# Latent x tiles loaded transposed and scaled by columns, in the token phase of a diffusion-transformer layer

## What is computed

```python
def rmsnorm(x, g):
    y = xf * lax.rsqrt(jnp.mean(xf * xf, axis=-1, keepdims=True) + EPS)
    return (y * g.astype(jnp.float32)).astype(x.dtype)

def modulate(x, g, shift, scale):
    return rmsnorm(x, g) * (1.0 + scale) + shift

h_lat = modulate(x, g_attn[i], sh1, sc1)
h_ctx = modulate(ctx, g_attn[i], csh1, csc1)
# project(): z = h @ w_in (1024 x 1184), split into cq, ckv, kr, qs, ks, vs;
# q_m = rmsnorm(cq) @ w_uq, kv = rmsnorm(ckv) @ w_ukv, RMS norms and rotary on q and k
```

## Time and profile before

| what | us |
|---|---|
| median of 3 timed runs | 1397.72 (1397.13 to 1399.58) |
| profiled execution | 1399.78 |
| its span (first to last instruction) | 1398.0 |
| TensorE busy | 1357.5 |
| VectorE busy | 914.6 |
| ScalarE busy | 692.6 |
| GpSimd busy | 487.1 |

### The profile page before, as it was taken

The page is one execution under the profiler, slowest core; times in us unless marked ns, Lnnn a source line. Parts: engine busy times, 40 slices in busy tenths (PEclk is TensorE's granted clock), DMA queues, the critical chain, the costliest instruction groups (busy, mean ns, idle before and its releaser), DMA issues.

```text
span 1398.0 us, 18825 instructions
## 1 busy us (share of the span) xinstructions
PE 1357.5 (97%) x7262; PEld 1149.4 (82%) x7262; DVE 914.6 (65%) x1284; ACT 692.6 (50%) x1343; POOL 487.1 (35%) x321
## 2 busy tenths in 40 slices
PE   5899997999999999999999999999999999999999
PEld 1688987999899988988887888888888888888887
DVE  1878776777777877875774646547564654746463
ACT  2755655788778777972223424333332433333240
POOL 2766553121299992501102303132050323205010
PEclk8999998999999999999999999999999999999999
DMA  9555658433365646301123112121211212121013
GB/s 377 192 162 160 177 159 286 129 89 86 115 199 144 190 131 191 71 1 61 31 76 121 31 31 90 31 75 31 62 44 30 91 31 75 30 62 44 15 61 121
DMA packets 121576, 143.42 MB, mean 103 GB/s; under 512 B 8184, under 2 KB 103288, under 8 KB 118672
## 3 DMA queue, kind: packets, MB, share of 16 engines
q1 hardware_dynamic: 121232, 142.18, 32.6%
q0 software_dynamic: 256, 0.05, 0.0%
HBM read 108.38 MB, written 31.74 MB: 100 GB/s over the span
## 4 chain that ended last, share of the span: by engine, by line
PE 70%; DVE 11%; POOL 7%; ACT 6%; DMA 4%; issue 1%; SPq 1%; DVEq 0%; ACTq 0%; POOLq 0%
PE f_ps L2062 24%; PE f_ps L2331 19%; PE o_ps L1770 6%; PE a_ps L1422 4%; PE a_ps L1438 3%; PE f_ps L2347 3%; POOL l_wg L1349 3%; ACT s_pr L1519 3%; POOL l_gate L1351 3%; PE t_ps L956 2%; PE a_ps L1468 2%; DVE s_nmx L1604 2%; PE t_ps L945 1%; DMA t_wm<-in_w_mod 1%; DMA l_v<-scratch_v 1%
## 5 line engine op out<-in xcount | busy, mean ns | idle before, releaser
L2062 PE MATMUL f_ps<-h,f_w 128*128 128x512 f32 x1536 | 358.0, 389 | 0.4 <-DVE h L1836 0.2
L2062 PEld LDWEIGHTS f_ps<-h,f_w 128*128 128x128 f32 x1536 | 288.1, 188 | 60.7 <-DVE h L1836 0.7
L2261 DVE TENSOR_TENSOR mix<-mix,f_ps 128x512 f32<-128x512 f32 x196 | 128.7, 683 | 152.9 <-PE f_ps L2331 152.9
L2102 POOL TENSOR_TENSOR f_w<-f_w,f_g 128x1024 f32<-128x1024 f32 x30 | 77.0, 2590 | 390.2 <-DMA f_w<-in_w_mlp 342.7
L2139 ACT ACTIVATE f_a<-f_ps 128x512 f32<-128x512 f32 x64 | 38.2, 597 | 254.7 <-PE f_ps L2062 254.7
L2331 PE MATMUL f_ps<-f_bh,f_al 128*128 128x512 f32 x392 | 152.5, 389 | 0.0
L2331 PE MATMUL f_ps<-f_bh,f_ah 128*128 128x512 f32 x392 | 152.5, 389 | 0.0
L2331 PE MATMUL f_ps<-f_bl,f_ah 128*128 128x512 f32 x392 | 152.5, 389 | 0.0
L1618 DVE TENSOR_TENSOR l_pT<-a_ps,l_pT 128x512 fp32r<-128x512 f32 (+1 forms) x192 | 108.9, 594 | 54.0 <-ACT l_pT L1529 53.9
L1422 PE MATMUL a_ps<-l_k,l_q 96*128 96x512 f32 (+1 forms) x576 | 136.5, 366 | 1.6 <-DMA l_v<-scratch_v 1.1
L956 PE MATMUL t_ps<-w_in,t_h 128*128 128x416 f32 (+2 forms) x600 | 125.7, 355 | 0.3 <-DVE w_in L719 0.3
(11 more groups left out here) (223 smaller groups left out, 2425.1 us busy)
## 6 DMA issues: line engine op xcount, KB each, us to landing
l_wg<-in_w_mod SPq DMA_DIRECT2D x8, 2048.0 KB, 8.0
f_w1r<-in_w_mlp SPq DMA_DIRECT2D x32, 512.0 KB, 4.0
f_w<-in_w_mlp SPq DMA_DIRECT2D x16, 1024.0 KB, 5.0
t_wm<-in_w_mod SPq DMA_DIRECT2D x8, 1024.0 KB, 12.5
scratch_k<-t_kT SPq DMA_DIRECT2D x20, 384.0 KB, 3.7
l_k<-scratch_k SPq DMA_DIRECT2D x8, 960.0 KB, 10.6
scratch_q<-t_qT SPq DMA_DIRECT2D x16, 384.0 KB, 3.9
l_q<-scratch_q SPq DMA_DIRECT2D x8, 768.0 KB, 6.3
```

The lines of the kernel that those rows point to most:

```text
L2062: last = nc.tensor.matmul(ps[:, b, :], w1[:, g % 2, w, k, :], h2[x][:, k, half * HB:(half + 1) * HB], start=(k == 0 and i == 0), stop=(k = ...
L2261: V.tensor_tensor(x, x, ps[:, bank_of(i, t), :].rearrange("p (k c) -> p k c", c=P), ALU.add).then_inc(added, 1)
```

## The change

Context tiles keep their way. Latent tiles (t >= 2) change:

- The host adds an input `x_cols`, x per tile with the model dimension on partitions (8 blocks of 128x128). SP loads it into `xT[t % 2]` (`load_xT`, `next_xT`); the plain x is still loaded for its squares.
- TensorE doesn't turn x. Its fill "x" is one 128x128 matmul that turns a broadcast of the inverse-RMS column, so that the inverse stands along columns in every partition. It stands behind the first k of chunk 1, before "s"; before, "x0" and "x1" stood behind chunk 2.
- VectorE scales `xT` in eight instructions of 128 columns, one for each block, by a per-partition scale from `mods` and the inverse row in PSUM; the last one counts `emptied`. It later makes the low part from SBUF in one instruction of 1024 (`low_x`), into `lT[t % 2]`.
- GpSimd adds the shift from `mods`, broadcast along columns. ScalarE makes the high part from SBUF in one instruction of 1024 (`high_x`), in `hT[t % 2]`; `project` waits for `h_lo`.
- The latent scale and shift rows are not spread; four transposes of `mo` and one copy make `mods` (128x16).
- In turn 1, `scale_x(2)` moves from behind `inverses(0)` to behind `c_variances(1)`.
- The stores at the program's end count one semaphore, not four.

```diff
@@ -253,16 +258,19 @@
     slot = {}
     for i in range(-1, NT + 1):
         order = [("sk", 0), ("k0", 0), ("k1", 0)] if i == NCT else []
-        order += ([("s", i - 1)] if lat(i - 1) else []) + [("sk", i - 1)] if i > 1 else []
-        turned = [(k, i - 1) for k in (("k0", "k1", "q0", "q1") if lat(i - 1) else ("k0", "k1"))] if i > 1 else []
         here = [("c", i)] if 0 <= i < NT else []
-        order += here + turned if lat(i) else turned + here
-        order += [("x0", i + 1), ("x1", i + 1)] if i + 1 < NT else []
+        ahead = [("x", i + 1)] if 0 < i < NT - 1 else []
+        if i < 2:
+            order += here + ahead + ([("x0", i + 1), ("x1", i + 1)] if i < 1 else [])
+        else:
+            order += ahead + ([("s", i - 1)] if lat(i - 1) else []) + [("sk", i - 1)] + here
+            order += [(k, i - 1) for k in (("k0", "k1", "q0", "q1") if lat(i - 1) else ("k0", "k1"))]
         for f in order:
             slot[f] = len(slot)
 
-
-    spread_bank = (5, 6, 7, 3, 4, 5, 6, 7)
+    read_at = {f: n for n, f in enumerate(f for f in slot if f[0] != "x")}
+    spread_bank = (5, 6, 7, 3)
+    MB = 4
     JOBS = ["a0", "a1", "kv", "r0", "r1", "r2", "r3", "uq"]
     kv_bank = lambda t: UB if t == 1 else UB + 2
 
...
@@ -342,8 +353,16 @@
             sp.dma_start(wm[k], A["w_mod"][0, k * P:(k + 1) * P, 0:2 * D]).then_inc(wm_loaded[k], 16)
 
         def next_x(i):
-            sp.wait_ge(emptied, slot["x1", i] + 1)
+            sp.wait_ge(x_squared, i + 1)
+            if i < NCT:
+                sp.wait_ge(emptied, slot["x1", i] + 1)
             load_x(i + 2)
+
+        def next_xT(i):
+            sp.wait_ge(z_ready, z_at(i) + (3 if lat(i) else 1))
+            if i:
+                sp.wait_ge(xT_loaded, 16 * i)
+            load_xT(i + 2)
 
         sp.dma_start(cc[:, :, :], A["c_cols"]).then_inc(c_loaded, 16)
         sp.dma_start(ident[:, :], A["ident"]).then_inc(ident_loaded, 16)
...
@@ -403,13 +427,15 @@
             return tmp
 
         def add_shift(t):
-            pool.wait_ge(h_scaled, t)
-            if t == 1:
-                pool.wait_ge(spread_copied, 4)
-            if t == NCT:
-                pool.wait_ge(spread_copied, 8)
-            shift = shift_l if lat(t) else shift_c
-            G.tensor_tensor(xr[:, t % 2, :], xr[:, t % 2, :], shift[:, :], ALU.add).then_inc(h_ready, 1)
+            if lat(t):
+                pool.wait_ge(emptied, slot["x", t] + 1)
+            else:
+                pool.wait_ge(h_scaled, t)
+            if lat(t):
+                G.tensor_tensor(xT[t % 2][:, :, :], xT[t % 2][:, :, :], bc(mods[:, 0:8], P), ALU.add).then_inc(h_ready, 1)
+                return
+            pool.wait_ge(spread_copied, 4)
+            G.tensor_tensor(xr[:, t % 2, :], xr[:, t % 2, :], shift_c[:, :], ALU.add).then_inc(h_ready, 1)
 
         def rotate_keys(t):
 
...
@@ -505,12 +531,15 @@
 
         def copy_spread(n):
 
-            dst = (scale_l, shift_l)[n % 2] if n >= 4 else (scale_c, shift_c)[n % 2]
+            dst = (scale_c, shift_c)[n % 2]
             f = n // 2 % 2
             act.wait_ge(spread, n + 1)
-            if n < 4:
-                act.wait_ge(h0_ready, n // 2 + 1)
+            act.wait_ge(h0_ready, n // 2 + 1)
             nc.scalar.activation(dst[:, f * BANK:f * BANK + BANK], ps[:, spread_bank[n], :], ACT.Copy).then_inc(spread_copied, 1)
+
+        def high_x(t):
+            act.wait_ge(h_ready, t)
+            nc.scalar.activation(hT[t % 2][:, :, :], xT[t % 2][:, :, :], ACT.Copy).then_inc(h_hi, 1)
 
         def hi_fill(kind, t):
             n = slot[kind, t]
...
@@ -663,14 +689,19 @@
                     att.first_exp()
                 if lat(i - 1):
                     hi_fill("q0", i - 1)
-                    hi_fill("q1", i - 1)
+            if 1 < i < NT - 1:
+                high_x(i + 1)
+            if i > 1 and lat(i - 1):
+                hi_fill("q1", i - 1)
             if i < NT and not lat(i):
                 hi_fill("c", i)
             if lat(i) and i < NT:
                 copy_z(i, 2)
-            if i + 1 < NT:
-                hi_fill("x0", i + 1)
-                hi_fill("x1", i + 1)
+            if i == 0:
+                hi_fill("x0", 1)
+                hi_fill("x1", 1)
+            if i == 1:
+                high_x(2)
             if i == 0:
                 square_x(2, stn[:, 0, 26:27])
             if i == 1:
...
@@ -687,14 +718,22 @@
         link = Chain(dve, v_chain)
 
         def scale_x(t):
-            r = stx[:, t:t + 1] if t < 2 else inv[:, (t - 2) % 2, 26:27]
-            scale = scale_l if lat(t) else scale_c
-            if t == 1:
-                dve.wait_ge(spread_copied, 4)
-            if t == NCT:
-                dve.wait_ge(spread_copied, 8)
-            V.scalar_tensor_tensor(out=xr[:, t % 2, :], in0=xr[:, t % 2, :], scalar=r, in1=scale[:, :],
+            if lat(t):
+                dve.wait_ge(filled, slot["x", t] + 1)
+                dve.wait_ge(xT_loaded, 16 * (LATS(t) + 1))
+                for k in range(KC):
+                    x = xT[t % 2][:, k, :]
+                    ins = V.scalar_tensor_tensor(out=x, in0=x, scalar=mods[:, 8 + k:9 + k], in1=ps[:, slot["x", t] % 2, 0:P],
+                                                 op0=ALU.mult, op1=ALU.mult)
+                ins.then_inc(emptied, 1)
+                return
+            dve.wait_ge(spread_copied, 4)
+            V.scalar_tensor_tensor(out=xr[:, t % 2, :], in0=xr[:, t % 2, :], scalar=stx[:, t:t + 1], in1=scale_c[:, :],
                                    op0=ALU.mult, op1=ALU.mult).then_inc(h_scaled, 1)
+
+        def low_x(t):
+            dve.wait_ge(h_hi, t - 1)
+            V.tensor_tensor(lT[t % 2][:, :, :], xT[t % 2][:, :, :], hT[t % 2][:, :, :].bitcast(F32), ALU.subtract).then_inc(h_lo, 1)
 
         def modulate_first():
 
...
@@ -863,8 +905,6 @@
                 link.reach()
                 variances(i - 1)
                 inverses(i - 1)
-                if i == 1:
-                    scale_x(2)
                 scale_s(i - 1)
                 if lat(i - 1):
                     scale_q(i - 1)
...
@@ -900,9 +940,13 @@
             if i < NT and not lat(i):
                 lo_fill("c", i)
                 c_variances(i)
-            if i + 1 < NT:
-                lo_fill("x0", i + 1)
-                lo_fill("x1", i + 1)
+            if i == 0:
+                lo_fill("x0", 1)
+                lo_fill("x1", 1)
+            if i == 1:
+                scale_x(2)
+            if 0 < i < NT - 1:
+                low_x(i + 1)
             if i == 0:
                 low_weights("r0")
             if i == 1:
...
@@ -919,7 +963,10 @@
             n = slot[kind, t]
             if n >= 2:
                 pe.wait_ge(emptied, n - 1)
-            if kind[0] == "x":
+            if kind == "x":
+                pe.wait_ge(inv_ready, t - 1)
+                parts = [inv[:, (t - 2) % 2, 26:27].to_broadcast([P, P])]
+            elif kind[0] == "x":
                 f = int(kind[1])
                 if t:
                     pe.wait_ge(h_ready, t)
...
@@ -1025,32 +1074,31 @@
         project_first()
         for i in range(NT + 1):
             if 0 < i < NT:
-                pe.wait_ge(emptied, slot["x1", i] + 1)
+                if lat(i):
+                    pe.wait_ge(h_lo, i - 1)
+                else:
+                    pe.wait_ge(emptied, slot["x1", i] + 1)
                 project(i, 0, {1: ("sk", 0), 3: ("k0", 0), 5: ("k1", 0)} if i == NCT else {})
-            if i == 0:
-                for n in range(4, 8):
-                    spread_row(n)
             if i < NT and not lat(i):
                 fill("c", i)
-                fill("x0", i + 1)
-                fill("x1", i + 1)
                 if i == 0:
+                    fill("x0", 1)
+                    fill("x1", 1)
                     pe.wait_ge(w_lo, JOBS.index("kv"))
-                    pe.wait_ge(spread_copied, 8)
+                else:
+                    fill("x", 2)
                 pe.wait_ge(emptied, slot["c", i] + 1)
                 up_kv(i)
             elif i < NT:
                 if i == NCT:
                     pe.wait_ge(w_lo, JOBS.index("r3"))
+                ahead = {0: ("x", i + 1)} if i + 1 < NT else {}
                 if lat(i - 1):
-                    project(i, 1, {2: ("s", i - 1), 5: ("sk", i - 1)})
+                    project(i, 1, ahead | {2: ("s", i - 1), 5: ("sk", i - 1)})
                     project(i, 2, {1: ("c", i), 2: ("k0", i - 1), 3: ("k1", i - 1), 4: ("q0", i - 1), 6: ("q1", i - 1)})
                 else:
-                    project(i, 1, {4: ("sk", i - 1)})
+                    project(i, 1, ahead | {4: ("sk", i - 1)})
                     project(i, 2, {1: ("c", i), 3: ("k0", i - 1), 5: ("k1", i - 1)})
-                if i + 1 < NT:
-                    fill("x0", i + 1)
-                    fill("x1", i + 1)
                 pe.wait_ge(emptied, slot["c", i] + 1)
                 if i == NCT:
```

53 lines of the change are left out of this document (33 added, 20 removed).

## The result

The changed kernel takes 1407.73 us (median of 4 runs, 1406.67 to 1409.96), the kernel before 1398.65 us beside it (1397.13 to 1399.74). The ratio is 1.0068, with a 95% interval of 1.0053 to 1.0083: slower by 9.1 us, where 5.6 were forecast, inside the range. The span of the profiled run is 1408.0 us (before 1398.0), its mean granted clock 0.987 (0.988).

The account below looks back on a forecast made before the run. TensorE, busy for 97% of the span, was taken as the bound, with VectorE's queue on the path at the start. Start +3.5 and six tiles +2.1 gave +5.6 us on the median of 1397.72: 1403.3 us, range 1396.5 to 1410.

Parts of the forecast that it names:

- Sign and order of the causes: Token phase: slower by 5.6 us, +3.5 from the start and +2.1 from six tiles; chance of slower 0.69.
- The tile: Regular latent tiles: 1.15 us later for the sk wait, 0.81 earlier without transposes; +0.35 a tile, +2.1 for six.
- TensorE's q at 14.25 us in: Latent tile: TensorE's transposes of q come 14.25 us into the tile, which was 13.1.
- takes the same 2.38 us: Latent tile: GpSimd's shift of x was to keep its 2.38 us and start no later.
- Rival (a): Latent tiles: x emptied so early that sk never waits; tiles give 4.3 us, ending at 1394.9; chance 0.13.
- The start: Ahead of the regular tiles: the chain of scalings, shift, copy and subtraction delays `project(2, 0)`; +3.5 us (+1.5 to +5.5).
- I add 0.4 for the slow clock there and at 40 to 47 us: Start: TensorE's lower clock after idle ahead of `project(2, 0)` and at 40 to 47 us costs 0.4 us.
- SP is held no longer than before: nothing: SP's load queue: the added 512 KB `x_cols` load per tile, behind the spill of q, costs nothing.
- Less 0.8 for the transposes: Start, ahead of `project(3, 0)`: the removed transposes save 0.8 us, bringing the delay from +3.9 to +3.1.
- Rival (d): Latent tiles: the 1.3 us wait lowers TensorE's clock, 2 us more a tile, total 1415; chance 0.07.
- the nearer row: Earlier trace: an idle of 1.15 us left the clock at 1.00; nearer to the tile's 1.3 than the 2.00 us idle.
- Rival (c): Tile's end: VectorE's subtraction of 1024 meets GpSimd's rotation of q, say 0.8 us a tile, total 1408; chance 0.11.

Follow-up runs that it names:

- e5_warm: Changed kernel plus eight 128x512 matmuls that nobody reads in TensorE's idle ahead of `project(2, 0)`; ratio 1.0048 to the kernel before.
- c0_again: The changed kernel run once more, unchanged; ratio 1.0060 to the kernel before.
- e2_x2_early: Changed kernel with x(2)'s inverse filled inside `project(1, 0)` and x(2) scaled before the low half of v(0); ratio 1.0035 to the kernel before.
- e10_hold: e9_tail plus twelve matmuls that nobody reads in the first stage; ratio 1.0014 to the kernel before.
- e9_tail: Changed kernel with x(2)'s scaling, x(3)'s load and c(1) earlier, unread spreads restored, other moves, tile scalings ahead of k's scaling; ratio 0.9997 to the kernel before.

## Why the forecast was right, and where it was short

**Sign and order of the causes: right.** Both places were named, and both mechanisms are in the trace as written: the two-bank wait of sk in six tiles, and the chain of scalings, shift, copy and subtraction ahead of `project(2, 0)`.

**The tile: +0.35 forecast, +0.46 found.** The scalings span 2.15 us (2.2 forecast), sk stands 8.54 us into the tile (8.5), and the wait is 1.15 us (1.3), since the spread inverse and the rest put TensorE there at 7.4 and not at 7.2. The step that was short is "TensorE's q at 14.25 us in": it stands at 14.45 and waits 0.29 us for k's low parts. ScalarE begins k0 at 12.58 (12.5 forecast), copies for 0.84 us to 166.86; VectorE begins at 166.96 and has two parts done at 167.82, TensorE begins at 167.89. The hand-overs between engines, about 0.1 us each, were left out of the sum. Over the six tiles it is +2.5 us where +2.1 was forecast, since one tile of before took 20.55.

**GpSimd's shift "takes the same 2.38 us": wrong, by luck harmless.** It took 1.90 us with the shift read as eight broadcast columns instead of a full second tensor. VectorE's work beside it isn't the reason: next to the same low part of w_uq it took 2.37 us before (at 71.78) and 1.90 after (at 81.65). At the start this is 0.5 us less on the chain; in the tile nobody waits for it.

**The low part of vs.** Rival (a) rested on VectorE and GpSimd holding each other up less. They do (0.33 us instead of 1.86), but the time comes free behind the scalings, where VectorE then waits for ScalarE's c: it could not help sk.

**The start: +3.5 forecast, about +6.2 found.** From `project_first` to `project(2, 0)` the sum was nearly right: 27.64 us in both traces of the changed kernel, 23.46 and 23.48 in those of before, +4.2 where +3.9 was forecast. The chain itself, from the low part of c(1) to `project(2, 0)`, took 7.2 us where 7.6 were forecast, by the shorter shift; but this low part came 20.44 us behind `project_first` and not 19.79, 0.2 of that because `project(1, 0)` started later behind the slow `up_kv(0)`. What was short lies behind it, where the forecast had 0.8 less and the traces have +2.0 (27.0 us in the mean of three, 25.0 of two):
- "I add 0.4 for the slow clock there and at 40 to 47 us". e5_warm shows about 2 us at the first place alone. The fall of the clock was foreseen from the earlier trace rows, but not over how much work: it covered a whole first projection of 8.26 us, which took 5.5 at full clock. Of that, what is lost against before is less, as said above.
- "SP is held no longer than before: nothing". The new load of x(3) stands in SyncE's queue behind the spills of tile 0, which wait for VectorE. VectorE waits 0.75 us for it (1.51 in c0_again, 1.92 in e2_x2_early), and c's wait behind it, 1.37 and 2.14 us, falls to 0.57 once the load is moved: 0.8 us or more.
- "Less 0.8 for the transposes": TensorE has this work less, and more idle than it saved. How the +2.0 splits between the clock and the load is not shown: the kernel before alone spreads by 1.6 us over this stretch (25.79 and 24.18).

**The clock in the tiles.** Rival (d) did not come: the granted clock over tile 6 is 1.00, with an idle of 1.15 us in each tile; behind the idles of 2.44 and 3.92 us at the start it was 0.50. So the nearer row was the right one, though idle alone doesn't decide: in the changed kernel an idle of 2.29 us at 75.56 left the clock at 1.00. The Trainium skill ("TensorE: Matmul & The Clock Gate", A second HAM failure mode) warns of short idles between groups of matmuls; at this spacing the trace does not show it. Rival (c) did not come either: the subtraction of 1024 (L736) took 1.22 us in every tile.

**Eight small instructions.** The Trainium skill ("VectorE: DVE Perf Modes", section on the TRN2 errata) asks for 512 elements or more per instruction. The eight of 128 took 343 ns each and 2.15 us together against 1.37 for the one of 1024 that they replaced, so the trace agrees: 0.8 us more, in a place where TensorE waits for it.

## What to carry to other kernels

Where producers and consumers share two banks, a step taken out of the filling engine is worth nothing if the step that comes in its place leaves its bank later: look who empties it, and move that work ahead of what nobody waits for (here 0.87 us, one line). When a wait is moved away, ask what the next fill waits for, since the next edit of the same kind may only move it on (0.37 us ahead of sk became 0.33 ahead of c). Price each new load by its place in the queue that issues it. For each new idle of about 2 us on TensorE, put half clock over all of the work behind it among the rivals: here it came behind some of these idles and not behind others. And trace a kernel twice before crediting 1 or 2 us in a start like this one to an edit.

## What the runs showed of the hardware

- Where the half clock falls in the first stage differs between runs of one program (before: the same four spreads in 3.67 and 5.16 us). Over all kernels the spreads took 3.67 us in two traces and 5.1 to 6.7 us in eleven (e10_hold left out), and `project_first` moves by up to 3.4 us with it. A start is better compared from a step behind it.
- An add of 1024 elements on GpSimd took 1.90 us with eight columns, each broadcast, as its second input, and 2.39 with a full tensor.
- An idle of 1.15 us in every tile left the clock at 1.00. Idles of 1.4 and 2.04 us in a row, where the spreads had been, were followed by half clock in all seven traces that have them, and in none of the seven with the spreads in their place. Single idles near 2 us went either way: behind 2.29 us (changed kernel, at 75.56) and 2.36 and 2.14 us (c0_again, at 75.37 and 82.19) the clock stayed at 1.00, behind 2.39 us in e9_tail's attention it fell (0.71 from 494 to 498), and at the same place in the changed kernel behind 2.19 us (0.50 from 501 to 503).
